# A norm by token tile, two weight tiles multiplied side by side, and output weights asked for one tile later

## The reference, cut to what matters

```
x = x + hier_moe(rms_norm(x, g_ffn), ...)        # end of the first layer
h = rmsnorm(x, norm_mix[0])                       # x / sqrt(mean(x*x) + eps), times a gain per column
y = h @ ev_w_in                                   # 1024 x 3048: the second projection
qa_nope, qa_rope, c_kv, ka_rope, iq, ik, iw, qb, kb, vb = split_cols(y, EVEN_SPLITS)
c_kv = rmsnorm(c_kv, kv_gain); k_nope = c_kv @ w_uk; v = c_kv @ w_uv
score = sum over heads of iw * relu(iq @ ik)      # the 64 best keys of each query are chosen
...                                               # rope on qa_rope, ka_rope, iq, ik, qb, kb; two attentions
mix = concat([o_a, o_b]) @ ev_w_out               # the output weights
```

## Time and profile before

| | us |
|---|---|
| median of three runs | 1046.19 |
| lowest, highest | 1043.50, 1049.99 |
| profiled execution, its own time | 1046.07 |
| its span | 1044.3 |
| PE busy, share of the span | 966.1, 93% |
| DVE busy | 591.0, 57% |
| ACT busy | 480.6, 46% |
| POOL busy | 122.7, 12% |

### The profile page before, as it was taken

One profiled execution on the slowest core, in us unless ns is written; L12 is line 12 of the kernel. 1 busy time (PEld: TensorE's weight loads), 2 busy tenths in 40 slices (PEclk: granted clock), 3 DMA queues, 4 the chain that ended last, 5 costly groups with the idle time before them and its releaser, 6 DMA issues.

```text
span 1044.3 us, 20523 instructions
## 1 busy us (share of the span) xinstructions
PE 966.1 (93%) x8706; PEld 693.7 (66%) x8706; DVE 591.0 (57%) x933; ACT 480.6 (46%) x826; POOL 122.7 (12%) x140
## 2 busy tenths in 40 slices
PE   6999999999767678999999999999999999999996
PEld 5776896554333335886668777776986558777774
DVE  5677888621000004899765645454888856544553
ACT  5556652410000006765665535436657765453442
POOL 6510550000000001032010000000043400000000
PEclk9999999999988899999999999999999999999998
DMA  8746119999999997666045575673725034756611
GB/s 263 238 144 218 43 43 375 389 420 421 421 421 421 420 410 254 229 218 195 1 167 190 178 236 177 190 243 116 243 89 162 2 139 129 242 167 230 225 57 41
DMA packets 109371, 228.81 MB, mean 219 GB/s; under 512 B 7353, under 2 KB 86635, under 8 KB 94827
## 3 DMA queue, kind: packets, MB, share of 16 engines
q1 hardware_dynamic: 106411, 219.78, 58.2%
q0 software_dynamic: 2880, 7.88, 2.6%
HBM read 224.76 MB, written 1.05 MB: 216 GB/s over the span
## 4 chain that ended last, share of the span: by engine, by line
PE 63%; DMA 13%; DVE 10%; ACT 3%; issue 1%; POOL 1%; SPq 0%; DVEq 0%; POOLq 0%
PE later_pB L926 20%; PE later_pB L935 10%; DMA ring<-in_w_down 6%; DMA ring<-in_w_gate 5%; PE later_pB L882 4%; PE later_pB L386 4%; PE rw_pB L1415 3%; DVE field L300 2%; PE later_pB L914 2%; PE rw_pB L1436 2%; PE rw_pB L2491 2%; DMA wt<-in_ev_w_in 1%; PE rw_pB L1444 1%; PE later_pB L4076 1%; PE later_pB L4062 1%
## 5 line engine op out<-in xcount | busy, mean ns | idle before, releaser
L926 PE MATMUL later_pB<-field 128*128 128x256 f16 x1920 | 212.9, 273 | 0.0
L926 PEld LDWEIGHTS later_pB<-field 128*128 128x128 f16 x1920 | 187.8, 98 | 25.5
L755 DVE SCALAR_TENSOR_TENSOR field<-field 128x2048 f16<-128x2048 f32 x84 | 153.9, 1869 | 57.2 <-ACT field L650 57.2
L650 ACT ACTIVATE field<-field 128x2048 f16<-128x2048 f32 x84 | 126.4, 1567 | 15.9 <-DMA field<-in_ffn_w_up 9.7
L935 PE MATMUL later_pB<-field 128*128 128x512 f16 x528 | 117.7, 379 | 0.6 <-DVE field L755 0.6
L386 PE MATMUL later_pB<-field 128*128 128x256 f16 (+2 forms) x960 | 114.9, 274 | 0.6
L386 PEld LDWEIGHTS later_pB<-field 128*128 128x128 f16 x960 | 94.2, 99 | 13.5 <-ACT field L322 1.8
L935 PEld LDWEIGHTS later_pB<-field 128*128 128x128 f16 x528 | 51.5, 98 | 58.9 <-issue 1.5
L1415 PE MATMUL rw_pB<-ring,kept 128*32 128x256 f32 x736 | 65.6, 420 | 18.7 <-DMA ring<-in_w_up 14.8
L1352 DVE TENSOR_TENSOR rw_mu_a<-rw_pB,rw_mu_a 128x256 f32<-128x256 f32 x8 | 3.4, 425 | 119.3 <-PE rw_pB L1415 119.3
L771 DVE SCALAR_TENSOR_TENSOR field<-later_pB,field 128x512 f32<-128x512 f32 x22 | 15.2, 691 | 91.5 <-ACT field L668 91.5
(11 more groups left out here) (606 smaller groups left out, 1630.6 us busy)
## 6 DMA issues: line engine op xcount, KB each, us to landing
ring<-in_w_gate SPq DMA_DIRECT2D x24, 1024.0 KB, 22.0
ring<-in_w_down SPq DMA_DIRECT2D x23, 1024.0 KB, 26.4
ring<-in_w_up SPq DMA_DIRECT2D x22, 1024.0 KB, 26.2
field<-in_ffn_w_down SPq DMA_DIRECT2D x22, 1024.0 KB, 5.0
field<-in_ffn_w_gate SPq DMA_DIRECT2D x20, 1024.0 KB, 7.7
field<-in_ffn_w_up SPq DMA_DIRECT2D x20, 1024.0 KB, 9.9
wt<-in_ev_w_in SPq DMA_DIRECT2D x9, 1024.0 KB, 5.7
wt<-in_od_w_in SPq DMA_DIRECT2D x9, 1024.0 KB, 5.6
```

Source lines behind the costliest of these rows:

```text
L650: copy = lambda o, i, scale=1.0: nc.scalar.activation(o, i, ACT.Copy, scale=scale)
L755: return nc.vector.scalar_tensor_tensor(out, whole, scale, hi, ALU.mult, ALU.subtract)
L926: ins = T.matmul(p[:, s, j * SEQ:(j + 1) * SEQ], w[:, s, m, c, j::NJ], h[:, c, :], start=(n == 0), stop=(n == 3 * KC - 1))
```

## The change

Token tile 0 gets its mean, root and scaling as soon as its own squares are there; token tile 1 is scaled half by ACT, half by DVE (`row_left`, `rows_ready`). PE issues six unread products instead of ten and turns token tile 0 when it is ready, then tile 1; it gives `moe_done`, for which POOL waits before it clears semaphores and issues its five requests, only after these transposes. ACT does not make the high part of weight tile 1 any more; DVE does, ahead of the low part of tile 0. PE's first two tiles are one list: the chunks of term 0 of both tiles interleaved (tile 1 two chunks behind), then the rest of tile 0 with the order 2, 1, then the rest of tile 1. The gain is asked for behind both first weight tiles. All output weight pieces are asked for and split one k later. The latent turn goes from after 14 to after 35 of the 48 matmuls of tile 2.

```
     def first_loads(self, sp):
         for k, (at, n) in enumerate(self.tiles[:2]):
             sp.dma_start(self.wt[:, k, :, 0:n], ...).then_inc(self.w_in[k], 16)
-            if k == 0:
-                sp.dma_start(self.gcol[:], cols(self.gain)).then_inc(self.gain_in, 16)
+        sp.dma_start(self.gcol[:], cols(self.gain)).then_inc(self.gain_in, 16)
...
+    def begin_two_act(self, act):
+        act.wait_ge(self.gain_in, 16)
+        for c in range(KC):
+            act.wait_ge(self.turned, c // 2 + 1)
+            self.nc.scalar.activation(self.sT_hi[:, c, :], self.pT[...], ACT.Copy, scale=self.gcol[:, c:c + 1]).then_inc(self.high_T, 1)
+    def begin_two_dve(self, dve):
+        n = self.tiles[1][1]
+        dve.wait_ge(self.hi_ready, 1)
+        dve.wait_ge(*self.raw_in_of(1))
+        self.nc.vector.tensor_scalar(self.w_hi[:, 1, :, 0:n], self.wt[:, 1, :, 0:n], W_SCALE, None, ALU.mult).then_inc(self.hi_ready, 1)
+        dve.wait_ge(self.hi_ready, 2)
+        self.begin_dve(dve)
+    def multiply_two(self, pe):
...
+        pe.wait_ge(self.hi_ready, 1)
+        for c in range(KC + 2):
+            if c < KC:
+                pe.wait_ge(self.high_T, c + 1)
+                add(0, c, 0, c == 0, False)          # one chunk, both token tiles
+            if c == 2:
+                pe.wait_ge(self.hi_ready, 2)
+            if c >= 2:
+                add(1, c - 2, 0, c == 2, False)
+        for k, order in enumerate(((2, 1), (1, 2))):
+            for term in order:
+                if term == 2:
+                    pe.wait_ge(self.lo_ready, k + 1)
+                for c in range(KC):
+                    if k == 0 and term == 1:
+                        pe.wait_ge(self.low_T, c + 1)
+                    ins = add(k, c, term, False, term == order[-1] and c == KC - 1)
+            ins.then_inc(self.product, 1)
...                                                     # PE, end of the expert layer
-            stream(T, pB[:, 0, 0:3 * P], keep.marks[:, 0:P], keep.marks[:], 10)
-            pe.wait_ge(rows_ready, TT)
+            stream(T, pB[:, 0, 0:3 * P], keep.marks[:, 0:P], keep.marks[:], 6)
+            following["turn"](pe, ((rows_ready, 1),), 0)
+            following["turn"](pe, ((rows_ready, 2), (row_left, 1)), 1)
...                                                     # ACT
-            act.wait_ge(end_recips, 1)
-            nc.scalar.activation(x_st[:, 2, :], x_st[:, 1, :], ACT.Sqrt).then_inc(end_roots, 1)
-            act.wait_ge(end_roots, 1)
-            copy(out[:, 1, :], x[:, 1, :], x_st[:, 2, 1:2]).then_inc(rows_ready, 1)
+            for t in range(TT):
+                act.wait_ge(end_recips, t + 1)
+                nc.scalar.activation(x_st[:, 2, t:t + 1], x_st[:, 1, t:t + 1], ACT.Sqrt).then_inc(end_roots, 1)
+            act.wait_ge(end_roots, 2)
+            copy(out[:, 1, 0:512], x[:, 1, 0:512], x_st[:, 2, 1:2]).then_inc(row_left, 1)
...                                                     # DVE
+            for t in range(TT):
+                dve.wait_ge(end_squares, len(X_ORDER) - TT + t + 1)
+                ...                                     # sum, mean, reciprocal of token tile t
             dve.wait_ge(end_roots, 1)
             vec.tensor_scalar(out[:, 0, :], x[:, 0, :], x_st[:, 2, 0:1], None, ALU.mult).then_inc(rows_ready, 1)
+            dve.wait_ge(end_roots, 2)
+            vec.tensor_scalar(out[:, 1, 512:], x[:, 1, 512:], x_st[:, 2, 1:2], None, ALU.mult).then_inc(rows_ready, 1)
...
-EVEN_LOADS, EVEN_HIGHS = {2: (0, 1), 3: (2, 3), 5: (4,), 6: (5,), 7: (6,), 8: (7,)}, {1: (0, 1), 2: (2, 3), 4: (4,), 5: (5,), 6: (6,), 7: (7,)}
-EVEN_LOWS, LATE_LOWS = {1: (0, 1), 2: (2,), 3: (3,), 4: (4,), 5: (5,)}, (6, 7)
+EVEN_LOADS, EVEN_HIGHS = {3: (0, 1), 4: (2, 3), 6: (4,), 7: (5,), 8: (6,), 9: (7,)}, {2: (0, 1), 3: (2, 3), 5: (4,), 6: (5,), 7: (6,), 8: (7,)}
+EVEN_LOWS, LATE_LOWS = {2: (0, 1), 3: (2,), 4: (3,), 5: (4,), 6: (5,)}, (6, 7)
...
         def turn_latent(done):
-            if done == 5:
+            if done == 26:
```

48 lines of the change are left out of this document (35 added, 13 removed).

## The result

The changed kernel takes 1050.2 us (median of 18 runs) against 1046.7 for the kernel before (18 runs): ratio 1.0039, 95% interval 1.0029 to 1.0048, so by the ratio 4.1 us more (3.0 to 5.0). Forecast were 1.6 us more. The direction was right. Of the two places of the loss, one was forecast and too small, and the other, the landing of tile 2, had been put at nothing.

A forecast was written before the change was run, and what follows sets the result against it. PE's matmuls and DVE's list with POOL's rope behind it were taken to arrive together at the turn of kb, so PE's gain brings nothing. 1046.07 + 0 (Step 4) + 1.6 (Step 6) = 1047.7 us, range 1043.4 to 1050.2.

The forecast's parts named there:

- rival A: Projection front: PE's gain arrives at the end, 1043.7 us if all 2.4 us come through, or 1045.7; chance 0.25.
- Step 1: Norm by token tile ahead of the projection: PE's 16 transposes start and end 0.85 us earlier.
- Step 4: Tile 2 and moved output weights: tile 2 lands after 6.6 to 7 us; taken as 0, ends -0.4 and +1.3 us.
- Step 2: PE's tiles 0 and 1 side by side: chunk waits shrink; with the earlier transposes, 2.4 us gained on PE.
- Step 3: High part of weight tile 1 on DVE: taken as 1.35 us, hidden in DVE's free 3.03 us before 417.64.
- Step 5: Turn of the index queries near 439: PE, ahead by then, is held by DVE for some 0.9 us.
- Step 6: POOL's first rope, started earlier, meets about five of DVE's eight weighing instructions: +1.6 us, ends 0 and 2.8.
- C: Weighing beside POOL's rope: full collision, +2.8 us, with the landing of tile 2 at +0.4: 1049.3 us; chance 0.10.
- B: Whole kernel: nothing moves, landing of tile 2 and rope collision both at 0: 1046.1 us; chance 0.20.
- D: Turn of kb and first scores: clock falls at 483 after PE's gaps, +3.3 us on the forecast, 1051.0; chance 0.06.

The follow-up runs named there:

- x12: Changed kernel with the latent turn back after 14 of the 48 matmuls of tile 2; 1048.51 us, one run.
- x4: Changed kernel with the high part of weight tile 1 made by ACT ahead of the chunks, not by DVE; ratio 1.0027 to the kernel before.
- x13: Changed kernel with POOL's three small requests (two gains, lambda) held until tile 2 has landed, `uk` and `uv` left in front; ratio 1.0022 to the kernel before.
- x2: Changed kernel with the output weights asked for and split at their old places; ratio 1.0019 to the kernel before.
- x15: Changed kernel with the edits of x13 and x1 together; ratio 0.9983 to the kernel before.
- x1: Changed kernel with POOL's first rope held until DVE has made all four weighings; ratio 1.0003 to the kernel before.
- x9: Changed kernel with DVE's low part of output piece 5 moved behind the weighing at k = 7; ratio 1.0030 to the kernel before.
- x3: Changed kernel with all five POOL requests held until the low part of tile 0; ratio 1.0045 to the kernel before.
- x7: Changed kernel with the edits of x4 and x1 together; ratio 1.0008 to the kernel before.
- x8: Changed kernel with the edits of x4, x1 and x2 together; ratio 1.0008 to the kernel before.
- x5: Kernel before the change, with POOL's first rope held until DVE's four weighings are made; ratio 1.0006 to the kernel before.
- x10: Kernel before with only the norm by token tile, six unread products and the earlier turn; ratio 1.0002 to the kernel before.
- x14: Changed kernel with the edits of x13, x4 and x1 together; ratio 0.9994 to the kernel before.
- x6: Changed kernel with all five POOL requests held until tile 2 has landed; ratio 1.0069 to the kernel before.

## Why the prediction was right and wrong

**What bounds it: right.** PE's gain of the front did not arrive (rival A), because DVE's list and POOL's rope behind it set the end. x12, where PE waits 2.2 us at the latent turn and ends the same, shows it again.

**Step 1: right in kind for PE.** The first transpose starts 3.27 us after the anchor, before 3.81: 0.54 earlier, not 0.85. The six unread products start 2.29 us after the anchor, before 1.97: PE's issue took 1.02 us in front of them (0.71 before), where I had let them start as before. Wrong was that POOL's requests go out 1.1 us later; step 4 says what hung on it.

**Step 2: right.** 10.55 us for the 96 matmuls, no wait for a chunk among them above 0.2 us; they end 2.1 us earlier by the anchor (2.4 forecast). ACT's move behind the product of tile 0 starts 12.47 us after the anchor, before 12.89 (415.20): 0.4 earlier, taken 0.8.

**Step 3: right.** 1.18 us, taken 1.35, inside the bounds of 1.2 to 2.2 but for 0.02. It is hidden where I said. But through the request of tile 2 it was not free: in x4, without it, tile 2 is asked for 1.2 us sooner.

**Step 4: the step that failed.** "I take 6.6 to 7: landing at 415.7 to 416.1, within 414.5 to 417.2." It landed in 9.2 us, at 418.5. I had bounded the landing from above by the 8.1 us before. The request went out 1.2 us later by the anchor (6.51, before 5.28), near the 1.5 forecast; but the transfer, taken as 1.1 to 1.5 us shorter than before, was 1.1 longer. So tile 2 lands 2.3 us later, and the other 0.5 of the term arises right behind it, where DVE waits 1.79 us for ACT's high part of tile 3. The term, taken as 0 with an upper end of 1.3, measured 2.80. Both ways of taking it away (x4, x13) give the turn of kb 2.5 to 2.85 us.

Two premises failed. The first is the place of POOL's requests. They did not go out 1.1 us later but 0.3 earlier (4.37 us after the anchor, before 4.67), while the tile's request moved back; POOL's first is now 2.1 us ahead of the tile's, before 0.6. POOL's timeline before, then after:

```profile
406.98 0.81 POOL L3128 DMA_DIRECT2D field<-in_ev_w_uk  x1 [262.06 <-PEq L148]
```

```profile
407.14 0.81 POOL L3191 DMA_DIRECT2D field<-in_ev_w_uk  x1 [262.88 <-issue]
```

The second is whose the excess of 2.7 us is: I gave 0.6 to the output pieces and the rest to POOL's 640 KB as a whole. x2 shows the pieces at 0 (9.1 with, 9.2 without), x13 and x15 the three smallest requests at 2.2 to 3.4. The Trainium skill (DMA: Bandwidth & Descriptors, Queues, rings and completion order) was the better guide: by the estimate made from it, requests behind the tile cost nothing and the landing would be at 417. x2 agrees on the first, and the second was still 1.5 us short.

How far POOL's first request is ahead of the tile's, and the time to landing, in all profiles:

| lead of POOL's first, us | requests of POOL in flight beside the tile | us to landing of tile 2 |
|---|---|---|
| 2.1 | all five | 9.2 (changed), 9.3 (x1), 9.2 (x9), 8.9 (x12); 9.1 with two pieces behind (x2) |
| 0.2 behind it | all five | 9.5 (x3) |
| 0.9 | all five | 7.3 (x4, x7); 7.7 with two pieces behind (x8) |
| 0.6 to 0.8 | all five, two pieces behind | 8.1 (before), 7.7 (x5), 8.0 (x10) |
| 2.1 | `uk`, `uv` | 5.8 (x13), 7.0 (x15) |
| 0.9 | `uk`, `uv` | 6.8 (x14) |
| none | none | 7.0 (x6) |

My own times give a lead of 1.0 us (0.6 less 1.1 plus 1.5), and with 0.9 the tile did land in 7.3, near the 7 forecast. But x3, with POOL behind the tile, has 9.5, so the lead does not order the landings by itself. That the three small requests cost the tile much at a lead of 2.1 us is shown; why, and why only 0.5 us at 0.9 (7.3 against 6.8), stays open.

**Step 5: right.** PE waits 0.68 us there, 0.9 forecast.

**Step 6: right in mechanism, too small.** Taken +1.6 (3 x 0.95 less 1.2), measured +3.85 - 1.22 = 2.6, near the upper end of 2.8; holding the rope returns 2.67. I let five of eight instructions meet POOL; the chain of waits shows six (three pairs of 2.63 to 2.75 us behind a first of 0.7), so 4 x 0.95 = 3.8 more than before in place of 2.8. x1 shows that it is the collision: with the rope held the eight take 3.20 us. By the anchor POOL started 2.2 us later than my 460.3 (462.97 less 0.46), but the weighing 2.8 us later than before (461.94 against 459.11). The two terms are thus not quite independent: a late DVE lengthens the collision. The Trainium skill (SBUF — State Buffer, Who interferes with whom) calls it an exclusive lock for whole instructions. The trace agrees: POOL's six operations keep their 1.26 to 1.34 us, and a pair of weighing instructions among them takes 2.63 to 2.75 us in place of 0.76, as long as two of POOL's.

**The rivals.** The nearest was C, +3.2 us, given 0.10; the case that came, step 4 beyond its upper end and step 6 near it, had none of its own. B is excluded by the interval. **D** was wrong where I put it and not idle: behind PE's wait of 2.95 us the clock did fall, at 474 to 477, which the windows view of the changed kernel shows (clock in the third column from the end):

```profile
474.00:475.00 1.00, 1.00 (x6) 0.69 (x7) 0.90 (x5) 0.00 (x0) 0.00 (x0) 0.50 0.00 0
```

Sixteen matmuls took 3.48 us there. It cost 0.1 us at most, since PE would else have waited for POOL, whose rope ends at 488.92, just ahead of the turn at 489.05. And the half clock that the kernel before had at 513 was gone, -1.6 us, which I had not considered. By the profiles, 5.5 us were lost and 1.6 came back from there; without that the time would lie outside my range instead of at its end.

**Not settled:** why the clock falls at 511 to 522 in six profiles and not in ten. The turn of kb does not decide it (80.82 with and 81.33 without, but 85.36 with), nor does PE's list ahead of it in any way that I could name. Nor does an earlier fall decide it: between 402 and 511 us the clock falls once in the changed kernel, x1, x2, x6, x9 and x12, and of these x9 has the later dip too; in x3, x4, x5, x13 and x15 it falls nowhere up to 552. In x1 it falls at 420 to 424 us, in a stretch whose code is that of the changed kernel, which stays at 1.00 there; PE had waited 1.97 us in front of it in x1, 1.42 in the changed kernel. So the 1.6 us that came back are read from one execution of each kernel; that the timed loss (4.1 us) is near the 3.84 of the profiles is all that speaks for them.

## What to carry to other kernels

When a change moves a request, look at what small transfers are in flight with it on the other queue: 129 KB of them cost more here than 512 KB, so do not price them by kilobytes (nor, by x13, by count of pieces), but try the tile without them, and put element-wise and repeated rows behind the big tile that somebody waits for. When POOL and DVE both read SBUF, find the start of POOL's block in DVE's list and count the DVE instructions with two SBUF inputs under it; one wait that puts the block behind them can be worth more than the work moved. And a gain on an engine that is 99% busy is no gain until the chain of waits runs through it: here three steps did what they said, and with both losses taken out the turn of kb stands where it stood (80.82 in x14).

## What the runs showed of the hardware

- Three requests of 129 KB in all (two with one element for each partition, one with a row repeated 128 times) in flight with a 1 MB tile cost it 2.2 to 3.4 us: 9.2 against 7.0 (x15) and 5.8 us (x13) to landing; the DMA engines were 82 to 92% busy at 100 to 112 GB/s, without them in x13 93 to 94% at 230 to 273. The Trainium skill (DMA: Bandwidth & Descriptors, Specifications) gives 512 B as the least transfer for line rate. No run here tests that: of the three, one has rows of 1 KB, and `uv`, in pieces of 256 bytes, stayed beside the tile.
- The same three requests are in flight before the change as well, with POOL 0.6 us ahead of the tile instead of 2.1, and the DMA engines moved 270 to 375 GB/s from 411 to 413. There the tile took 8.1 us. So what they cost depends on when they meet the tile, by the table in step 4 not in proportion to their lead.
- Two 512 KB requests behind a tile on the same queue cost it nothing in x2 (9.1 and 9.2 us) and 0.4 us in x8 (7.7, against 7.3 in x7), no more than landings with the same requests differ by themselves (7.7 and 8.1, 5.8 and 7.0).
- The clock is no sure follower of a gap: behind a wait of 2.95 us it fell to 0.50 and 16 matmuls took 3.48 us; in x13, at the same place and behind 2.93 us, it stayed at 1.00 and they took 1.92. It also fell behind waits of 1.95 (x9), 1.97 (x1), 2.18 (x12) and 2.7 us (x2), and stayed behind 2.93 (x4), 2.52 and 2.32 us (x3). The timeline of x13:

```profile
471.39 1.92 PE L444 MATMUL later_pB<-field 128*128 128x256 f16 x16 [2.93 <-DVE field L299]
```
